# 32 instead of 16 dense tokens take U's activations from fetched rows, and the gate planes are made in another way (two-layer mLSTM / stick-breaking / PEER trunk)

## What is computed

```python
def block(args):
    xt, et, gt = args                      # tokens, their 128 experts each, their gates
    act = jax.nn.gelu(jnp.einsum("td,thkd->thk", xt, expert_u[et]), approximate=False) * gt
    return jnp.einsum("thk,thkd->td", act, expert_v[et])
```

## Time and profile before

| | us |
|---|---|
| median of three runs (lowest to highest) | 3004.49 (3003.03 to 3005.43) |
| the profiled execution | 3004.32 |
| its span, first to last instruction | 3002.6 |
| PE busy in the span | 2955.5 (98%) |
| DVE, ACT, POOL busy | 2583.3 (86%), 1532.5 (51%), 1663.7 (55%) |

### The profile page before, as it was taken

The page is one execution under the profiler, slowest core; times in us unless marked ns, Lnnn a source line. Parts: engine busy times, 40 slices in busy tenths (PEclk is TensorE's granted clock), DMA queues, the critical chain, the costliest instruction groups (busy, mean ns, idle before and its releaser), DMA issues.

```text
span 3002.6 us, 45274 instructions
## 1 busy us (share of the span) xinstructions
PE 2955.5 (98%) x15514; PEld 2623.5 (87%) x15514; DVE 2583.3 (86%) x5067; ACT 1532.5 (51%) x2866; POOL 1663.7 (55%) x1010
## 2 busy tenths in 40 slices
...
GB/s 272 240 110 101 89 159 216 361 335 387 368 353 386 390 394 391 393 388 381 198 223 154 117 68 85 135 201 331 352 369 372 366 378 387 387 378 370 344 352 230
DMA packets 327201, 863.94 MB, mean 288 GB/s; under 512 B 30480, under 2 KB 151328, under 8 KB 326992
## 3 DMA queue, kind: packets, MB, share of 16 engines
...
## 4 chain that ended last, share of the span: by engine, by line
PE 65%; DVE 21%; ACT 4%; issue 4%; DMA 3%; POOL 3%; ACTq 0%; DVEq 0%; POOLq 0%; SPq 0%
PE banks L1368 23%; PE gbank L1368 11%; PE banks L1348 5%; PE banks L1349 5%; PE banks L1350 5%; PE banks L1328 3%; PE banks L1330 3%; PE banks L1329 3%; DVE u_rows L2331 2%; POOL w_lo L724 2%; DVE hot L2302 2%; DVE pick L2259 2%; DVE pick L2254 1%; DMA raw<-stream_dram 1%; PE gbank L1727 1%
## 5 line engine op out<-in xcount | busy, mean ns | idle before, releaser
L724 POOL TENSOR_TENSOR w_lo<-raw,w_hi 128x1024 fp32r<-128x1024 f32 x355 | 910.0, 2567 | 485.8 <-ACT w_hi L827 482.3
L827 ACT ACTIVATE w_hi<-raw 128x1024 fp32r<-128x1024 f32 x613 | 646.4, 1055 | 583.8 <-PE banks L1368 328.1
L754 POOL DMA_INDIRECT v_rows<-v_dram,row_of x256 | 369.3, 1443 | 596.2 <-DVE fetched L2345 582.0
L1348 PE MATMUL banks<-h_hi,w_hi 128*128 128x368 f32 x2048 | 675.2, 330 | 0.0
L1349 PE MATMUL banks<-h_lo,w_hi 128*128 128x368 f32 x2048 | 672.9, 329 | 0.0
L1350 PE MATMUL banks<-h_hi,w_lo 128*128 128x368 f32 x2048 | 672.9, 329 | 0.0
L1348 PEld LDWEIGHTS banks<-h_hi,w_hi 128*128 128x128 f32 x2048 | 384.4, 188 | 1.6 <-POOL w_lo L724 0.8
L1349 PEld LDWEIGHTS banks<-h_lo,w_hi 128*128 128x128 f32 x2048 | 384.3, 188 | 0.0
L1350 PEld LDWEIGHTS banks<-h_hi,w_lo 128*128 128x128 f32 x2048 | 384.1, 188 | 0.0
L746 POOL DMA_INDIRECT u_rows<-u_dram,row_of x256 | 257.3, 1005 | 164.1 <-DVE z L2331 127.9
L2345 DVE SCALAR_TENSOR_TENSOR fetched<-v_rows,share,fetched 128x1024 f32<-128x1024 f32 x254 | 326.2, 1284 | 2.9 <-DMA v_rows<-v_dram,row_of 2.5
...
## 6 DMA issues: line engine op xcount, KB each, us to landing
...
```

What stands on the lines that cost most here:

```text
L724: pool.tensor_tensor(w_lo[:, s, :], raw[:, s, :], w_hi[:, s, :].bitcast(F32), ALU.subtract).then_inc(split_lo, 1)
L754: pool.indirect_dma_start(v_rows[:, j % V_ROWS, :], None, (v0, v1)[layer], bass.IndirectOffsetOnAxis(ap=row_of[:, j:j + 1], axis=0)).then_ ...
L827: act.activation(w_hi[:, s, :], raw[:, s, :], ACT.Copy).then_inc(split_hi, 1)
L1348: pe.matmul(out, wh, h_hi[:, k, 0:DENSE_U], start=(k == 0), stop=False)
```

## The change

More tokens are extra: `EXTRA` is 32, so U's dense product has 352 columns, 32 sums a layer are for extra tokens, and U has 160 sums, 4 in 3 tiles. The transposed gates of the extra tokens then fill whole 32 x 32 blocks, so that DVE's transpose writes them where they are used, and the eight small DMAs that gathered them (L634) go. The quad's `hot` has only the first key's one-hots. The high plane is made by four instructions, one a token, that compare the key numbers with the second key and multiply with the gate. ACT makes the low plane from the high one, times low part over high part; the quotient is made once for all gates (`low_share`). The sums beside the V stage are 26 instead of 15, and the conditioning dots are put at other tiles.

```diff
-EXTRA = 16
+EXTRA = 32
-    return range(min(U_SUMS, 23 * (n - ROWS_FROM) // 18), min(U_SUMS, 23 * (n - ROWS_FROM + 1) // 18))
+    return range(min(U_SUMS, 4 * (n - ROWS_FROM) // 3), min(U_SUMS, 4 * (n - ROWS_FROM + 1) // 3))
-EXTRA_GEL, EXTRA_TURN, EXTRA_LOAD, EXTRA_HI, EXTRA_LO = (EXTRA_DONE + n for n in (2, 4, 13, 26, 28))
+EXTRA_GEL, EXTRA_TURN, EXTRA_HI, EXTRA_LO = (EXTRA_DONE + n for n in (2, 4, 6, 8))
-V_DOT_EVERY = 6
+def dot_tile(i):
+
+    return 2 + 7 * i // 2
+def mod_dot_tile(i):
+
+    return 2 + 8 * i if i < 12 else 98 + 4 * (i - 12)
...
-            for q in range(GROUPS_OF_PICKS):
-                gather_extra(layer, q)
-                load_after(done_to + q)
...
             def low_planes(q):
...
-                act.wait_ge(S("hot"), past["hot"] + q + 1)
+                act.wait_ge(S("one"), past["one"] + q + 1)
                 for u in range(QUAD):
-                    last = act.activation(plane[:, q % 2, u, 1, :], hot[:, q % 2, 1, u, :].bitcast(F32), ACT.Copy,
+                    last = act.activation(plane[:, q % 2, u, 1, :], plane[:, q % 2, u, 0, :].bitcast(F32), ACT.Copy,
                                           scale=gate_lo[:, QUAD * q + u:QUAD * q + u + 1])
...
-            dve.tensor_tensor(gate_lo[:], misc[2][:, 0:DENSE_T], gate_hi.bitcast(F32), ALU.subtract
-                              ).then_inc(S("gate_lo"), 1)
+            def low_share(low, high, divisor):
+
+                dve.scalar_tensor_tensor(out=divisor, in0=high, scalar=0.0, in1=high, op0=ALU.is_equal, op1=ALU.add)
+                link(dve.tensor_tensor(low, low, high, ALU.subtract))
+                link(dve.reciprocal(divisor, divisor))
+                return dve.tensor_tensor(low, low, divisor, ALU.mult)
+
+            link(dve.tensor_copy(gate_lo[:], misc[2][:, 0:DENSE_T]))
+            low_share(gate_lo[:], gate_hi[:].bitcast(F32), stage[:, 0, 0:DENSE_T // BATCH, :].rearrange("p e t -> p (e t)")
+                      ).then_inc(S("gate_lo"), 1)
...
-                dve.tensor_tensor(hot[:, q % 2], keys_at.unsqueeze(1).unsqueeze(1).to_broadcast(full),
-                                  exT[:, 0:2, tok].unsqueeze(3).to_broadcast(full),
-                                  ALU.is_equal).then_inc(S("hot"), 1)
-                dve.wait_ge(S("hot"), past["hot"] + q + 1)
-                wide = [P, QUAD, NKEYS]
-                dve.tensor_tensor(plane[:, q % 2, :, 0, :], hot[:, q % 2, 1].bitcast(F32),
-                                  high_part[:, tok].unsqueeze(2).to_broadcast(wide), ALU.mult
-                                  ).then_inc(S("one"), 1)
+                dve.tensor_tensor(hot[:, q % 2], keys_at.unsqueeze(1).to_broadcast(full),
+                                  exT[:, 0, tok].unsqueeze(2).to_broadcast(full), ALU.is_equal)
+                for u in range(QUAD):
+                    one = slice(QUAD * q + u, QUAD * q + u + 1)
+                    last = dve.tensor_scalar(plane[:, q % 2, u, 0, :], keys_at, exT[:, 1, one],
+                                             gate_hi[:, one].bitcast(F32), ALU.is_equal, ALU.mult)
+                last.then_inc(S("one"), 1)
...
-                    dve.tensor_tensor(gate_lo[:, DENSE_U:], gate_extra, gate_extra_hi[:].bitcast(F32), ALU.subtract
-                                      ).then_inc(S("extra_by_dve"), 1)
+                    link(dve.tensor_copy(gate_lo[:, DENSE_U:], gate_extra[:]))
+                    low_share(gate_lo[:, DENSE_U:], gate_extra_hi[:].bitcast(F32), h_extra[:, 0:EXTRA]
+                              ).then_inc(S("extra_by_dve"), 1)
```

More of the change, by code:

```diff
@@ L111 @@
 assert quad_step(EXTRA_QUAD - 2) > DC * EXTRA_LO
-V_DOT_EVERY = 6
+def dot_tile(i):
+    return 2 + 7 * i // 2
 def dot_beside(v):
-    i, r = divmod(v - 2, V_DOT_EVERY)
-    return U_DOTS + i if r == 0 and 0 <= i < PICKS - U_DOTS else None
-Z_AT = V_DOT_EVERY * (PICKS - U_DOTS - 1) + 4
+    beside = [U_DOTS + i for i in range(PICKS - U_DOTS) if dot_tile(i) == v]
+    return beside[0] if beside else None
+def mod_dot_tile(i):
+    return 2 + 8 * i if i < 12 else 98 + 4 * (i - 12)
+Z_AT = dot_tile(PICKS - U_DOTS - 1) + 2
 assert Z_AT < Z_HALF
@@ L421, in build @@
     gate_lo = sb("gate_lo", [P, DENSE_T])
-    hot = sb("hot", [P, 2, 2, QUAD, NKEYS], F32R)
-    gate_hi = hot[:, 0, 0].rearrange("p t e -> p (t e)")[:, 0:DENSE_T]
+    hot = sb("hot", [P, 2, QUAD, NKEYS], F32R)
     place[0] = max(place[0], ranked_end)
@@ L1123, in peer @@
                 act.activation(exT[:, n, :], misc[n][:, 0:DENSE_T], ACT.Copy).then_inc(S("exT"), 1)
[L1124 removed]
+            act.activation(gate_hi[:], misc[2][:, 0:DENSE_T], ACT.Copy).then_inc(S("exT"), 1)
             act.activation(keys_at, iota[:], ACT.Copy).then_inc(S("exT"), 1)
[L1126 to L1127 removed]
             def low_planes(q):
@@ L1172, in peer @@
                     act.wait_ge(S("dotted"), past["dotted"] + EXTRA_FROM + EXTRA)
-                    act.activation(z_extra[:, 0:EXTRA], z_extra[:, 0:EXTRA], ACT.Gelu).then_inc(S("extra_by_act"), 1)
+                    act.activation(z_extra[:], z_extra[:], ACT.Gelu).then_inc(S("extra_by_act"), 1)
                 if n == EXTRA_HI:
-                    act.wait_ge(S("extra_moved"), past["extra_moved"] + EXTRA_OUT)
-                    act.activation(gate_extra_hi[:], gate_extra, ACT.Copy).then_inc(S("extra_by_act"), 1)
+                    act.wait_ge(S("extra_by_dve"), past["extra_by_dve"] + GATES_TURNED)
+                    act.activation(gate_extra_hi[:], gate_extra[:], ACT.Copy).then_inc(S("extra_by_act"), 1)
                 for i in range(PIECES):
@@ L1203, in peer @@
                     a_high(n)
-                if layer == 0 and v % 6 == 0 and v // 6 < V_DOTS:
-                    v_ada_load(v // 6)
+                if layer == 0:
+                    for i in range(V_DOTS):
+                        if mod_dot_tile(i) == v + 2:
+                            v_ada_load(i)
             def summed(c):
@@ L1726, in gate_pair @@
                     u = PAIR * (p % 2) + t
-                    last = pe.matmul(pair_sums[p % 3][:, t].rearrange("p n e -> p (n e)"), hot[:, q % 2, 0, u, :],
+                    last = pe.matmul(pair_sums[p % 3][:, t].rearrange("p n e -> p (n e)"), hot[:, q % 2, u, :],
                                      plane[:, q % 2, u].rearrange("p n e -> p (n e)"), start=True, stop=True)
```

43 lines of the change are left out of this document (16 added, 27 removed).

## The result

| | before | changed |
|---|---|---|
| median, us (lowest to highest) | 3003.76 (3002.63 to 3005.43) | 3051.62 (3045.8 to 3063.44) |
| ratio of the two, with its 95% interval | | 1.0161 (1.0148 to 1.0174) |
| the profiled execution, us (span) | 3004.32 (3002.6) | 3063.44 (3061.7) |

The change makes the kernel 48 us slower, where 9 more were forecast.

The account below looks back on a forecast made before the run. PE, busy 98% of the span, was taken as the bound. Columns -16.0, start +5.0, loop with slower sums +12.0, smaller parts +2.2, times two layers, plus V 2.8, gave +9.2 on 3004.32: 3013.5, range 2988 to 3034.

Parts of the forecast that it names:

- Columns, 16.0 a layer: U tiles 28 to 127: 16 columns fewer save 0.16 us a tile, 16.0 us less a layer.
- The loop: Even-first U tiles: ACT and DVE's loop grows from 4.14 to 4.69 us a quad, over PE's 4.40; 10 us a layer.
- loop at its longest: Rival, even-first U tiles: 0.7 us of delay, no lead, 21.6 a layer, late start and V larger too; 3039, chance 0.09.
- Lock of DVE and POOL: Rival, 24 U tiles: `w_lo`, fetches and sums run in a row, 25.5 us more a layer; 3040, chance 0.03.
- slower sums: First even-first stretch of U: a second sum runs at 1.91 instead of 1.21 ahead of `gates_out`; 2 us a layer.
- POOL's pace: Rival, first even-first stretch: POOL needs 4.77 a tile against 4.32, 6.3 us a layer; 3002, chance 0.13.
- The start, 5.0: Tile 26: more DVE work, a reciprocal of 2.5 included, ahead of the first gate pair; 5.0 us more a layer.
- the 0.8 for the queue on ACT: Tile 26: low planes, `w_hi`, Gelu and the `h_extra` copy queue on ACT; about 0.8 us of the start's 5.0.
- tiles 0 to 25 give nothing: U tiles 0 to 25: PE, done 4.2 us earlier, waits for the same DVE ranking; no gain.
- `EXTRA_LO`, 1.5: Small two-SBUF instructions ahead of `gates_out`: one or two stalls reach PE in part, 1.5 us a layer.
- V, 2.5 and 0.3: V stage: eleven more sums, 13.3 us of DVE a layer, cost 2.5 us in layer 0 and 0.3 in layer 1.

Follow-up runs that it names:

- e5: The change with `one` told after each token's instruction and the extra tokens' sums taking their second operand from PSUM: 3004.63 us, ratio 1.0002 to the kernel before.
- e1: The change, but `one` is told after each of the four DVE instructions and ACT makes each low plane at once: 3024.48 us, ratio 1.0071 to the kernel before.
- e2: The change, but the extra tokens' sums take their second operand from PSUM instead of SBUF: 3039.43 us, ratio 1.0124 to the kernel before.
- e7: The change with `one` told per token, extra tokens' sums spread, quotient split, `h_extra` copy ahead of tile 26's `w_hi` and Gelu: 3019.21 us, ratio 1.0044.
- e4: The kernel before with only the planes of the change, still 16 extra tokens and 368 columns: 3050.92 us, ratio 1.0157 to the kernel before.
- e13: The change, but the rows of U fetched beside the V stage are 32 elements wide: 3048.76 us.
- e14: The change, but the sums beside the V stage multiply 32 elements instead of 1024, rows still fetched whole: 3052.78 us.

## Why the prediction was wrong

It was right in direction and in the parts that it named; the sizes were too small, and one rival was ruled out by a wrong reading.

- **Columns, 16.0 a layer.** Right: tiles at 4.32, both stretches at 104.7 and 104.6 in e5.
- **The loop.** Right mechanism, term mis-sized. I took a spacing of 0.26 from instructions with one small operand; with two it is (1.36 - 0.40) / 3 = 0.32, and the last takes 0.40 instead of 0.335. So `one` is told after 0.60 + 3 x 0.32 + 0.40 = 1.96, not 1.72, the loop is 4.89, not 4.69, and a stretch loses 24 x 0.49 - 2.1 = 9.7, not 4.9; the second one, at 113.5, is 9.8 over 24 x 4.32. The rival "loop at its longest" (4.84) was nearly this, and I gave it 0.09. The whole effect is 27 us (e1), for which the sum had 20.
- **Lock of DVE and POOL.** The step that failed. The sum has 2 a layer for slower sums, and I gave the lock 0.03 because a sum at 632.73 took 1.21 beside a fetch. That row shows that a sum does not wait for a fetch; the other way round, the fetch at 631.86 took 1.76 because it waited for the sum ahead of it, and the pair that decides, a DVE instruction behind `w_lo`, was in the earlier trace rows (2431 ns) and not weighed. The 4.36 of "POOL's pace" has that wait of the fetch in it, too. The Trainium skill ("SBUF — State Buffer", Who interferes with whom) calls the shared port an exclusive lock; e2 agrees with it for sum and `w_lo` (3.41 = 2.31 + 1.1, and never over 1.233 with a PSUM operand). My price of it, 25.5 a layer, was too high, since only some of the sums meet a `w_lo` (their median is 1.254 in the change): it is 20 for both layers once the loop is gone (e1 to e5), 12 beside the loop (e2), against the 4 in the sum.
- **The start, 5.0.** The reciprocal was right (2.55 for 2.5). Too small was the 0.8 for the queue on ACT: PE's second wait, for `h_extra`, went from 0.42 to 2.05. Not foreseen were some 3 and 7 us at half the clock. 8 to 10 in place of 5 (e7). That tiles 0 to 25 give nothing holds where the ranking meets a `w_lo`; where it does not they gave 2.4 of their 4.2.
- **`EXTRA_LO`, 1.5.** In the change its cast met the end of a `w_lo` (1.28, in layer 1 1.61) and its last multiply none (0.19); in e4 they met two whole ones (5 to 6 us). That the term was about right in the change is luck.
- **V, 2.5 and 0.3.** Measured 5.6 and 1.6. For layer 0 the cause I named, DVE's time, was wrong: it is the transfers, whose rate I had called "under V's" for U and not looked at for V (e13, e14). For layer 1 it stays open.
- **Tiles 125 to 127** had no term and cost 1.7: ACT waits 3.99 for a weight tile there. That this too is the transfers was not tried by itself.

Together the loop, the lock and the start are some 27 + 20 + 14 to 17 = 61 to 64 us (the start is 14 without tiles 0 to 25), V and the tiles before it 11, against 32 from the columns: 40 to 43 of the 48. The sum had 20, 4, 10 and 2.8 for these four.
